# A Mamba-style mixer, a mixture of experts and four attention-like layers in fp32: five early steps of the second expert group get their own buffers, and one broadcast load is issued earlier

## The reference, cut to what matters

```python
def first_block(x, ...):
    hn = rmsnorm(h, norm_mix[i])
    h = h + hybrid_mixer(hn, w_in[i], ..., w_out[i])
    hn = rmsnorm(h, norm_ffn[i])
    h = h + hierarchical_moe(hn, w_router_group[i], w_router_expert[i],
                             w_gate[i], w_up[i], w_down[i])
    return rmsnorm(h, final_norm)

def run_block(args):           # one expert on its tokens
    xb, e = args
    return (jax.nn.silu(xb @ w_gate[e]) * (xb @ w_up[e])) @ w_down[e]

def reference(...):
    x = first_block(...)
    return second_block(x, ...)    # layers fox, gla, gdn, fox
```

## Time and profile before

| | |
|---|---|
| median of 3 runs | 1306.1 us (1304.75 to 1307.91) |
| span of the profiled execution | 1299.1 us |
| median of the runs less that span | 7.0 us |
| TensorE busy | 1128.9 us (87%) |
| VectorE busy | 644.4 us (50%) |
| ScalarE busy | 439.5 us (34%) |
| HBM read | 312.52 MB, 241 GB/s over the span |
| mean granted TensorE clock | 0.927 |

### The profile page before, as it was taken

How to read it: one execution, slowest core, us unless ns; L and a number is a source line. 1 busy time by engine, 2 the same in 40 slices (tenths; PEclk the granted TensorE clock), 3 DMA queues, 4 the chain that set the end, 5 groups by cost and what they waited for, 6 DMA issues and landing times.

```text
span 1299.1 us, 19661 instructions
## 1 busy us (share of the span) xinstructions
PE 1128.9 (87%) x8060; PEld 820.3 (63%) x8060; DVE 644.4 (50%) x1265; ACT 439.5 (34%) x691; POOL 8.1 (1%) x35
## 2 busy tenths in 40 slices
PE   8999889887677768686858999999999979799998
PEld 7999767542232313141415789897779868778897
DVE  6787578420101010110203777767467965656685
ACT  5554434100000000000002656546356653255563
POOL 1000000000000000000000000000000000000000
PEclk9999999897878878787879999999999989999999
DMA  8755345989999999999998983354325530056600
GB/s 300 206 194 195 130 146 197 402 341 409 409 410 410 410 410 410 410 410 410 410 410 307 281 249 130 130 180 144 130 69 187 176 89 4 1 123 179 225 25 33
DMA packets 120004, 314.65 MB, mean 242 GB/s; under 512 B 17139, under 2 KB 17386, under 8 KB 119674
## 3 DMA queue, kind: packets, MB, share of 16 engines
q1 hardware_dynamic: 116864, 310.78, 66.0%
q0 software_dynamic: 352, 2.11, 0.4%
q10 hardware_dynamic: 2714, 0.71, 0.3%
HBM read 312.52 MB, written 1.06 MB: 241 GB/s over the span
## 4 chain that ended last, share of the span: by engine, by line
PE 66%; DMA 20%; DVE 8%; ACT 3%; issue 2%; SPq 1%; ACTq 0%; DVEq 0%
DMA ring<-in_w_up 18%; PE bank L2242 7%; PE bank L2235 7%; PE bank L2239 7%; PE bank L2224 6%; PE bank L2221 6%; PE bank L2217 6%; PE bank L2532 5%; PE bank L2555 4%; PE bank L2517 3%; PE bank L2133 3%; DVE w_l L1194 1%; DMA ring<-in_w_down 1%; PE bank L2150 1%; PE bank L2637 1%
## 5 line engine op out<-in xcount | busy, mean ns | idle before, releaser
L1194 DVE TENSOR_TENSOR w_l<-ring,w_h 128x1024 fp32r<-128x1024 f32 x204 | 246.6, 1221 | 90.7 <-ACT w_h L666 88.9
L666 ACT ACTIVATE w_h<-ring 128x1024 fp32r<-128x1024 f32 x204 | 213.7, 1057 | 176.2 <-PE bank L2224 89.3
L2532 PE MATMUL bank<-ring,cm 128*32 128x512 f32 x960 | 161.7, 810 | 101.4 <-DMA ring<-in_w_gate 52.6
L2532 PEld LDWEIGHTS bank<-ring,cm 128*32 128x32 f32 x960 | 31.3, 129 | 225.2 <-DMA ring<-in_w_up 89.0
L2235 PE MATMUL bank<-w_h,hnT_h 128*128 128x512 f32 x480 | 135.9, 405 | 4.6 <-DVE cm L1821 1.9
L2242 PE MATMUL bank<-w_l,hnT_h 128*128 128x512 f32 x480 | 129.6, 392 | 4.9 <-DVE w_l L1194 4.9
L2239 PE MATMUL bank<-w_h,hnT_l 128*128 128x512 f32 x480 | 129.9, 393 | 0.0
L1668 DVE SCALAR_TENSOR_TENSOR cm<-cm,bank 128x512 f32<-128x512 f32 x8 | 5.5, 687 | 213.0 <-ACT cm L887 213.0
L2242 PEld LDWEIGHTS bank<-w_l,hnT_h 128*128 128x128 f32 x480 | 89.7, 188 | 26.6 <-DVE w_l L1194 7.6
L2239 PEld LDWEIGHTS bank<-w_h,hnT_l 128*128 128x128 f32 x480 | 91.0, 190 | 20.1 <-DVE hnT_l L1309 0.2
L2235 PEld LDWEIGHTS bank<-w_h,hnT_h 128*128 128x128 f32 x480 | 87.0, 190 | 24.7 <-issue 5.1
(11 more groups left out here) (442 smaller groups left out, 1352.8 us busy)
## 6 DMA issues: line engine op xcount, KB each, us to landing
ring<-in_w_down SPq DMA_DIRECT2D x62, 1024.0 KB, 15.8
ring<-in_w_gate SPq DMA_DIRECT2D x60, 1024.0 KB, 14.5
ring<-in_w_up SPq DMA_DIRECT2D x60, 1024.0 KB, 15.1
ring<-in_fox_w_in SPq DMA_DIRECT2D x32, 1024.0 KB, 11.4
ring<-in_w_in SPq DMA_DIRECT2D x22, 1024.0 KB, 7.8
ring<-in_gla_w_in SPq DMA_DIRECT2D x12, 1024.0 KB, 6.2
ring<-in_gdn_w_in SPq DMA_DIRECT2D x12, 1024.0 KB, 6.8
ring<-in_w_out SPq DMA_DIRECT2D x8, 1024.0 KB, 6.4
```

Of the source, the lines that this page charges most:

```text
L666: af(part(w_h, u, width), w, ACT.Copy).then_inc(s["high_ready"], 1)
L1194: v.tensor_tensor(part(w_l, u, width), w, part(w_h, u, width).bitcast(F32), ALU.subtract).then_inc(s["low_ready"], 1)
L2532: x = mm(bank[a][CAP * e:CAP * (e + 1), :], m_xg[:, 2 * b + r, CAP * e:CAP * (e + 1)], expert_of(w, e)[:, r * FF:(r + 1) * FF], start=(b = ...
```

## The change

Group 1's steps 13 to 17 (its up steps 1 to 5) go to the same five outside buffers as group 0's steps 4 to 8, in the same order. SyncE issues each of them after it has waited for the use of the group 0 step that has the same buffer (`ring_used` 5 to 9). The ring then has step 12 and steps 18 to 23 of group 1, and the numbering of ring loads (`RING_BASE`, `released`, `slot_value`) moves with it. TensorE has group 1 written out as well, and its loop runs over groups 2 to 7. Apart from that the load of `final_norm` is issued by ScalarE in the fifth turn of the mixer's loop of exponentials, after a wait for `out_low` to reach 4, and no longer between `half_sum("moe", 1)` and `router_copy(1)`.

```diff
+SECOND_BUFFERS = ("ring", 0, 1, 2, 3, 4, "ring", "ring", "ring", "ring", "ring", "ring")
+EARLY_BUFFERS = FIRST_BUFFERS + SECOND_BUFFERS
+EARLY_RING = [j for j in range(2 * MOE_STEPS) if EARLY_BUFFERS[j] == "ring"]
+EXTRA_LOADS = 2 * MOE_STEPS - len(EARLY_RING)
...
             e = n - RING_BASE["moe"]
-            return s["ring_used"], 1 + (FIRST_RING[e] if e < len(FIRST_RING) else e + EXTRA)
+            return s["ring_used"], 1 + (EARLY_RING[e] if e < len(EARLY_RING) else e + EXTRA_LOADS)
...
                         for j in FIRST_ISSUES if q == 0 else range(MOE_STEPS):
-                            k = FIRST_BUFFERS[j] if q == 0 else "ring"
-                            if k != "ring":
+                            k = EARLY_BUFFERS[q * MOE_STEPS + j]
+                            if k != "ring" and q:
+                                sp.wait_ge(s["ring_used"], 1 + FIRST_BUFFERS.index(k))
+                                for dst, src in moe_loads(extra[k], q, j):
+                                    sp.dma_start(dst, src).then_inc(extra_ready[k], 16)
+                            elif k != "ring":
...
                 if i in SC_UNITS_AFTER_EXP:
                     high(first + SC_UNITS_AFTER_EXP[i])
+                if i == 4:
+                    act.wait_ge(s["out_low"], PAIR_BASE["ssd"] + 4)
+                    act.dma_start(cmf[:, 40 * T:44 * T], final_norm.rearrange("(a d) -> a d", a=1).to_broadcast([P, D]))\
+                       .then_inc(s["fnorm_loaded"], 16)
...
             half_sum("moe", 1)
-
-            act.dma_start(cmf[:, 40 * T:44 * T], final_norm.rearrange("(a d) -> a d", a=1).to_broadcast([P, D]))\
-               .then_inc(s["fnorm_loaded"], 16)
             router_copy(1)
...
-            def first_slot(q, j):
-                k = FIRST_BUFFERS[j]
+            def early_slot(q, j):
+                k = EARLY_BUFFERS[q * MOE_STEPS + j]
                 if k != "ring":
-                    pe.wait_ge(extra_ready[k], 32)
+                    pe.wait_ge(extra_ready[k], 32 * (q + 1))
                     return extra[k]
-                n = RING_BASE["moe"] + FIRST_RING.index(j)
+                n = RING_BASE["moe"] + EARLY_RING.index(q * MOE_STEPS + j)
...
-            pe_quad(0, 0, 0, first_slot, s["ring_used"], range(KD // 2, KD))
+            pe_quad(0, 0, 0, early_slot, s["ring_used"], range(KD // 2, KD))
+            pe_quad(1, 1, 1, early_slot, s["ring_used"])
             pe.wait_ge(s["rt_passes"], 1)
             passes = pe.value_load(count_i[0:1, 0:1], min_val=1, max_val=T // CAP)
-            with pe.Fori(1, NQ) as q:
+            with pe.Fori(2, NQ) as q:
                 pe_quad(q, q, q, ring_slot, s["ring_used"])
```

More of the change, by code:

```diff
@@ L55 @@
 FIRST_ISSUES = (4, 0, 1, 5, 2, 3, 6, 7, 8, 9, 10, 11)
-FIRST_RING = [j for j in range(MOE_STEPS) if FIRST_BUFFERS[j] == "ring"]
+SECOND_BUFFERS = ("ring", 0, 1, 2, 3, 4, "ring", "ring", "ring", "ring", "ring", "ring")
+EARLY_BUFFERS = FIRST_BUFFERS + SECOND_BUFFERS
+EARLY_RING = [j for j in range(2 * MOE_STEPS) if EARLY_BUFFERS[j] == "ring"]
+EXTRA_LOADS = 2 * MOE_STEPS - len(EARLY_RING)
 VEC_A = [("ssd_conv_w", 48), ("ssd_conv_b", 12), ("ssd_norm", 8), ("sc_conv_w", 24), ("sc_norm", 8),
@@ L107 @@
         RING_BASE["moe"] = _n
-        _n += NQ * MOE_STEPS - EXTRA
+        _n += NQ * MOE_STEPS - EXTRA_LOADS
 ROWN = {}
@@ L2578, in ring_slot @@
             def ring_slot(q, j):
-                n = RING_BASE["moe"] + MOE_STEPS - EXTRA + j
-                pe.wait_ge(ready[n % SLOTS], (q - 1) * (32 * MOE_STEPS // SLOTS) + slot_value(n))
+                n = RING_BASE["moe"] + len(EARLY_RING) + j
+                pe.wait_ge(ready[n % SLOTS], (q - 2) * (32 * MOE_STEPS // SLOTS) + slot_value(n))
                 return ring_halves(n % SLOTS)
             gather(0, 1, range(KD // 2))
-            pe_quad(0, 0, 0, first_slot, s["ring_used"], range(KD // 2, KD))
+            pe_quad(0, 0, 0, early_slot, s["ring_used"], range(KD // 2, KD))
+            pe_quad(1, 1, 1, early_slot, s["ring_used"])
             pe.wait_ge(s["rt_passes"], 1)
             passes = pe.value_load(count_i[0:1, 0:1], min_val=1, max_val=T // CAP)
-            with pe.Fori(1, NQ) as q:
+            with pe.Fori(2, NQ) as q:
                 pe_quad(q, q, q, ring_slot, s["ring_used"])
```

## The result

The changed kernel takes 1295.4 us (median of 10 runs, 1292.9 to 1299.7), the kernel before 1305.0 us in the 10 runs beside it (1300.1 to 1307.9). The ratio is 0.9934, with a 95% interval of 0.9918 to 0.9951: 8.6 us less, between 6.4 and 10.7. The forecast was 1300.5 us, in a range of 1298.3 to 1304.0, and 5.6 us less.

A forecast was written before the change was run, and what follows sets the result against it. The expert stage was taken as bound by its weight stream at 410 GB/s, which ran dry for 5.6 us. Closing that hole, all other terms 0, gave 1306.1 - 5.6 = 1300.5 us, range 1298.3 to 1304.0.

The forecast's parts named there:

- SyncE's issues and the windows of 260 to 280: Expert stream, signs: SyncE issues from about 256 and again at 268.7; 400 GB/s or more in 260 to 280 us.
- the 296 to 297: Group 1, sign: TensorE's first wait on a load comes at 296 to 297 us instead of 290.
- it does nothing: Expert stream, rival: the hole was not the empty queue, or it reappears behind step 17; 1306 us, chance 0.02.
- a slot that comes back late behind step 17: Near the group's end, rival: a released slot reaches the stream late; with the low-clock case, about 1303.8 us, chance 0.09.
- The written-out group: TensorE's group 1 written out instead of looped: the same instructions run, taken as 0, covered by a 2.29 us wait.
- ScalarE's wait: Fifth exponential of the mixing: the awaited low half is done at 169.2, the exponential is near 181; idle time covers 0.39 us.
- The buffers' term of 5.6: Expert stream: issuing steps 13 to 17 early into the outside buffers closes the hole at 260 to 280 us, 5.6 us gained.
- The median of the three runs is 7.0 us above the span; it carries over: Whole kernel: the gap between profiled span and median run time stays 7.0 us, so 1306.1 - 5.6 gives 1300.5 us.
- The tail of the experts: Last group's gather and down steps: clock level may shift, range -0.6 to +2.3 us, taken as 0.
- the queue drains at 246.7 instead, the hole grows by 1.28 us, and the gain is 0: Small hole near 247 us: removing the norm's load only lengthens the wait for TensorE's first step; gain 0.
- rival 1: Expert stream: the norm's load counts too, its 1.28 us come back; 1299.2 us, chance 0.08.
- -1.3 us of the norm's load: Expert stream: bound on the gain from removing the final norm's load, between 0 and -1.3 us, taken as 0.

The follow-up runs named there:

- the issue held: The whole change, but SyncE holds the issues of steps 13 to 16 until step 9 is used; ratio 1.0003 against the kernel before.
- two buffers: The whole change with only steps 13 and 14 outside the ring, 15 to 17 in it; ratio 0.9954 against the kernel before, -6.0 us.
- the kernel with one buffer: The whole change with only step 13 outside the ring, steps 14 to 17 back in it; ratio 0.9959 against the kernel before, -5.3 us.
- the buffers alone: Five outside buffers for group 1, the final norm's load left at its old place; ratios 0.9970 and 0.9954 against the kernel before.
- two loads put in: Outside buffers without the norm's move, plus two unread 512 KB final_norm loads ahead of step 8's load; ratio 0.9985 against the kernel before.
- The load moved alone: The kernel before with only the final norm's load moved, group 1 all in the ring; ratio 0.9987 against the kernel before.

## Why the prediction was right and wrong

**The mechanism was right.** The loss was an empty queue between step 12's load and the next free slot. The early issue alone closes it (the issue held: 1.0003), and two buffers do it as well as five. SyncE's issues and the windows of 260 to 280 came as forecast. The step behind TensorE's first long wait starts at 295.13, 1 to 2 us sooner than the 296 to 297 that I had set. The rival "it does nothing" and the one of a slot that comes back late behind step 17 did not come about; the second shows in the kernel with one buffer. The written-out group, ScalarE's wait and its 0.35 us of issue cost nothing that shows: the exponential behind it still has 1.85 us of idle time ahead of it.

**Up to the last down step the sum was right, in part by luck.** The whole change gains, from (a) to (d) and between profiles with the same start, 5.2 to 6.2 us with an early one and 6.4 to 6.8 with a late one; the forecast was 5.6. The buffers' term of 5.6 is 6.2 late and 4.8 early. I had taken it from one profile with a late start and did not know that there was another kind.

**The step that failed: "The median of the three runs is 7.0 us above the span; it carries over".** It made the time of before and everything outside the stream a fixed sum, with no term and no range of its own. The time lies 5.1 us under the forecast. 1.1 of that is before itself, 1305.0 over ten runs in place of 1306.1 over three, and of the 7.0 us 5.3 were chance. The rest is that the runs give 7.0 to 8.6 us in three comparisons (the medians of the first even 9.6), against 5.2 to 6.8 us up to (d). The middles of these two ranges are some 2 us apart, their ends 0 to 3. Behind (d) no instruction was changed, but the stretch takes 596.8 us, within 0.1, in six of the fifteen profiles and 599.4 to 605.3 in the others, by where the clock falls, and 1.0 us of delay ahead of it cost 6.9. The norm's load even in full, and the tail, were inside the range (1298.3), so they can't have put the time below it. That the changed kernel ends its experts at a better moment fits all of this, the 1 run of 28 over 1300 us most of all, beside 14 of 24 with the buffers alone. But there is one profile of each set of runs, and how much of the gain it is stays open.

**A second step failed in one kind of start: "the queue drains at 246.7 instead, the hole grows by 1.28 us, and the gain is 0".** With a late start, as in the profile that it was read from, it holds. (c)-(a) is 82.3 with the load in its old place and 82.3, 82.4 and 82.0 without it, and the hole at 246 us and behind it is 1.9, 2.0 and 1.4 us without it. With an early start SyncE's next issue comes 20.9 us after (a) instead of 22.4, before has no small hole, and a queue that is 1.28 us shorter empties only for a part of that: 0.7, 0.3 and 0.8 us in the three profiles of the changed kernel. There the load gives back 0.4 to 1.3 us (82.1 to 81.7, 80.8 and 80.9), and two loads put in cost 2.6. I had taken TensorE's first step as a fixed end; it comes 18.9 us after (a) or 1.0 to 1.5 us later. In four of the five late starts the first gather took 3.36 to 3.68 us, in the fifth the matmuls ahead of it were slow. The Trainium skill (DMA: Bandwidth & Descriptors, "Issuing engines are not separate DMA queues") says that transfers started by different engines run on the same 16 DMA engines and interleave. I had written that down as rival 1 with a chance of 0.08. The trace agrees where nothing empties the queue: the added loads cost their bytes in full, 1.3 us each. The load moved alone, and every late start, gave nothing.

**The tail of the experts** was set at 0 within -0.6 to +2.3. In the profile after, the clock is at its upper level in the last gather, and from the last up step of the last group to the last down step it takes 20.5 us instead of 21.1: -0.6, the end of the range that I had given. But the second profile of before has 20.5 as well (679.08 to 699.55), so this is not the change's doing.

The profile's own sum: the stream starts 0.4 us earlier, as the mixing ended so much sooner in that execution (chance), (c)-(a) is 6.8 us shorter (88.5 to 81.7), and the rest of the experts 0.6: 7.9 us with rounding, against 5.6. This pair sets a late start beside an early one. 1.6 of the 6.8 us are what an early start alone gave before (88.5 to 86.9), so a large part of the 2.3 us that this pair shows beyond the forecast is chance.

**The range was too narrow** for two reasons that I could have known. The range of the runs of before (1304.8 to 1307.9, three of them) was taken as the spread of a time, though the profile was 5.3 us faster than their median; the spread of single executions is about 9 us (1299.0 to 1308.5 over all the runs). And the -1.3 us of the norm's load stood in the text as a bound, but the low end of the range reached 1298.3 with it and the tail together and left nothing for a stretch that can end 7 us sooner or later by itself.

## What to carry to other kernels

In a stage that is one long stream of loads, ask when the queue is empty, not how often the engine waits. It pays to issue just so many loads ahead that the queue lasts until the next buffer comes back; here two did what five did, as far as the runs can tell.

When a load is moved out of such a stream, its worth is its bytes, but only if the next thing that the stream waits for is the stream itself. Compare the two arrival times with their spread, and don't take a hole of half a microsecond in one profile for a fixed end.

Before a term of 1 us is believed, look at each place where the clock stands at its lower level: a matmul row of twice the usual time on the path is a term that can come out either way in the next execution. Look at a second profile of the kernel before where one can be had. And give what lies behind the change a range, too: a stretch of unchanged instructions can take several microseconds more or less by when it starts.

## What the runs showed of the hardware that was not expected

- The stretch behind the experts took 596.8 to 596.9 us in six profiles of five kernels, and otherwise 599.4 to 605.3, with the same instructions apart from the copies. A delay of 1.0 us ahead of it cost 6.9 us in the mean of 12 runs; one of 0.35 us cost nothing that could be told.
- A broadcast load of one row of 4 KB to 128 partitions lowers the total rate while it is in flight: 340 to 365 GB/s at 234 to 236 us in the five profiles with such a load in flight there, and 399 to 428 in the ten others. The 2 us behind it are back at 395 to 422 with one such load and at 354 with two more.
- SyncE can put two loads of 1 MB into an empty queue in 0.88 us. With several megabytes queued ahead most of its issues took 2.3 to 5.9 us for one or two loads, at no cost while nothing else waits behind SyncE.
